# Two-layer hybrid encoder trunk: residual with tokens on partitions, hand-over between sub-layers by token block, next sub-layer begun on half of the tokens

## The reference

```python
for l in range(DEPTH):
    f = swiglu(rms_norm(x, ffn1_pre_g[l]), ffn1_w_gate[l], ffn1_w_up[l], ffn1_w_down[l])
    x = x + 0.5 * rms_norm(f, ffn1_post_g[l])
    m = hybrid_mixer(rms_norm(x, mix_pre_g[l]), ...)      # MLA, GLA, retention, one output projection
    x = x + rms_norm(m, mix_post_g[l])
    f = swiglu(rms_norm(x, ffn2_pre_g[l]), ffn2_w_gate[l], ffn2_w_up[l], ffn2_w_down[l])
    x = x + 0.5 * rms_norm(f, ffn2_post_g[l])

def rms_norm(x, g):
    return x * lax.rsqrt(jnp.mean(x * x, axis=-1, keepdims=True) + EPS) * g
def swiglu(x, w_gate, w_up, w_down):
    return (jax.nn.silu(x @ w_gate) * (x @ w_up)) @ w_down
```

## Time and profile before

| | |
|---|---|
| Median of 3 runs | 2079.45 us (2075.5 to 2079.79) |
| Profiled execution | span 2078.5 us from first to last instruction; the runs' own times stand in the line above |
| TensorE products / weight loads busy | 97% / 78% |
| VectorE, ScalarE, POOL busy | 43%, 33%, 9% |
| Mean granted TensorE clock | 0.982 |
| Read from HBM | 172.79 MB, 84 GB/s over the span |

### The profile page before, as it was taken

The page is one execution under the profiler, slowest core; times in us unless marked ns, Lnnn a source line. Parts: engine busy times, 40 slices in busy tenths (PEclk is TensorE's granted clock), DMA queues, the critical chain, the costliest instruction groups (busy, mean ns, idle before and its releaser), DMA issues.

```text
span 2078.5 us, 25293 instructions
## 1 busy us (share of the span) xinstructions
PE 2020.5 (97%) x9540; PEld 1628.4 (78%) x9540; DVE 897.6 (43%) x1137; ACT 693.5 (33%) x901; POOL 179.4 (9%) x185
## 2 busy tenths in 40 slices
PE   7999999999999999999999999999999999999997
PEld 6888888696677888888778888886956778888885
DVE  3444422635445544431364444226354464444314
ACT  5322211524443423221252223124444343223212
POOL 2000000202222000000020000003032220000000
PEclk9999999999999999999999999999999999999998
DMA  4222222230012222222212222223200112222222
GB/s 165 102 83 98 101 101 92 90 109 21 1 42 81 82 101 99 85 98 101 102 62 102 86 96 101 101 95 115 72 11 21 41 61 102 101 101 93 89 101 81
DMA packets 26615, 176.01 MB, mean 85 GB/s; under 512 B 3330, under 2 KB 3492, under 8 KB 6308
## 3 DMA queue, kind: packets, MB, share of 16 engines
q1 hardware_dynamic: 25024, 170.03, 22.4%
q10 hardware_dynamic: 1508, 4.87, 0.7%
HBM read 172.79 MB, written 2.10 MB: 84 GB/s over the span
## 4 chain that ended last, share of the span: by engine, by line
issue 77%; PE 16%; POOL 5%; DVE 1%; ACT 1%; DMA 0%; POOLq 0%; SPq 0%; DVEq 0%; ACTq 0%
POOL xL L1474 3%; PE ps L365 2%; PE ps L367 2%; PE ps L366 2%; PE ps L600 1%; PE ps L707 1%; POOL rstd L1484 1%; PE ps L725 1%; PE ps L518 1%; PE ps L519 1%; PE ps L520 1%; PE ps L714 0%; PE ps L609 0%; PE ps L641 0%; PE ps L682 0%
## 5 line engine op out<-in xcount | busy, mean ns | idle before, releaser
L1115 DVE TENSOR_TENSOR WL<-raw,WH 128x2048 fp32r<-128x2048 f32 x152 | 348.3, 2292 | 722.7 <-ACT WH L836 722.7
L365 PE MATMUL ps<-xH,WH 128*128 128x512 f32 x1632 | 639.3, 392 | 0.0
L367 PE MATMUL ps<-xH,WL 128*128 128x512 f32 x1632 | 635.4, 389 | 0.0
L366 PE MATMUL ps<-xL,WH 128*128 128x512 f32 x1632 | 635.3, 389 | 0.0
L836 ACT ACTIVATE WH<-raw 128x2048 fp32r<-128x2048 f32 x156 | 298.8, 1915 | 675.1 <-PE ps L367 675.1
L367 PEld LDWEIGHTS ps<-xH,WL 128*128 128x128 f32 x1632 | 306.1, 188 | 64.8
L365 PEld LDWEIGHTS ps<-xH,WH 128*128 128x128 f32 x1632 | 306.1, 188 | 64.4 <-issue 1.0
L366 PEld LDWEIGHTS ps<-xL,WH 128*128 128x128 f32 x1632 | 306.2, 188 | 63.8 <-issue 1.0
L366 PE MATMUL ps<-hL,WH 128*128 (+1 forms) x704 | 273.9, 389 | 0.0
L367 PE MATMUL ps<-hH,WL 128*128 (+1 forms) x704 | 273.9, 389 | 0.0
L365 PE MATMUL ps<-hH,WH 128*128 (+1 forms) x704 | 273.9, 389 | 0.0
(11 more groups left out here) (224 smaller groups left out, 1712.4 us busy)
## 6 DMA issues: line engine op xcount, KB each, us to landing
raw<-stream SPq DMA_DIRECT2D x158, 1024.0 KB, 4.8
x<-x_in SPq DMA_DIRECT2D x4, 512.0 KB, 9.7
wq<-w_q_up ACTq DMA_DIRECT2D x4, 512.0 KB
out<-x SPq DMA_DIRECT2D x8, 256.0 KB, 2.1
const<-consts ACTq DMA_DIRECT2D x2, 578.5 KB
wkv<-w_kv_up ACTq DMA_DIRECT2D x2, 512.0 KB
cos<-positions ACTq DMA_DIRECT2D x2, 256.0 KB
gains_all<-gains_in SPq DMA_DIRECT2D x1, 79.5 KB, 4.9
```

The lines of the kernel that those rows point to most:

```text
L365: mm(dst, wh, xh, start=start, stop=False)
L366: mm(dst, wh, xl, start=False, stop=False)
L367: return mm(dst, wl, xh, start=False, stop=stop)
L1115: tt(WL[:, slot, :], raw[:, slot, :], WH[:, slot, :].bitcast(F32), ALU.subtract).then_inc(wL_ready, 1)
```

## The change

The residual now has tokens on partitions: x is 4 blocks of 128 tokens by 1024 features. The down and output projections swap operands (hidden tile stationary, weights moving), so that two banks hold one token block. The mean of squares is then a sum along a row, which ScalarE's square delivers with it; POOL takes the power of one column per block; `residual` and `normed` scale by a column and by a gain row that a transfer has repeated over all partitions. Each normed block is turned by 8 transposes (`turn_block`) into two banks, from which ScalarE and VectorE make xH and xL (`high_x`, `low_x`). The next norm is fully applied ahead of the projections, so the multiplications by rstd_x go, and with them `columns`, the spreads of the eight outer norms, and `busy`.

The last two pairs of a sub-layer run together, output bank by output bank (`last_pairs`), so that token blocks are finished one after the other. The next sub-layer's first two pairs run on the first half of the tokens and then on the second (`enter`, `half_pair`), with the turns of blocks 2 and 3 in between. A third weight slot, used by pair base alone (`slot_of`), lies over gate, up and other tiles that rest at that time. Both layers are written out instead of looped. x comes in and leaves as 4 blocks. The core of the diff, with "..." where lines are left out:

```diff
-FFN_START = [2, 3, 6, 7, 4, 5, 0, 1]
+FFN_START = [6, 7, 2, 3, 4, 5, 0, 1]
...
+def slot_of(i):
+    return 2 if i == 0 else (i - 1) % 2
...
+            def load_norm_gains(k):
+                for j, row in enumerate((2 * k, 2 * k + 1)):
+                    if 0 < row < 2 * STAGES + 1:
+                        sp.dma_start(norm_g[:, j, :], norm_gains[row].partition_broadcast(P)).then_inc(norm_g_landed, 16)
+            sp.dma_start(x[:, 0, :], x_in[:, 0, :]).then_inc(x_landed[0], 16)
+            load_norm_gains(0)
+            sp.dma_start(ident[:], consts[:, C_ID:C_ID + P]).then_inc(ident_landed, 16)
+            sp.dma_start(x[:, 1, :], x_in[:, 1, :]).then_inc(x_landed[1], 16)
+            load_pair(0)
+            for b in range(2, BLK):
+                sp.dma_start(x[:, b, :], x_in[:, b, :]).then_inc(x_landed[b], 16)
+            load_pair(1)
...
+            for stage in range(STAGES):
+                base, pairs = first_pair_of(stage), MIX_PAIRS if stage % 3 == 1 else FFN_PAIRS
+                for p in range(base, base + pairs):
+                    if p < 2:
+                        continue
+                    sp.wait_ge(wH_ready, p - 1)
+                    sp.wait_ge(wL_ready, p - 1)
+                    if p == base + FT + 6:
+                        sp.wait_ge(pair_done, base + FT + 2)
+                        load_norm_gains(stage + 1)
+                    load_pair(p)
+                if stage % 3 == 1:
+                    sp.wait_ge(q_psum, HEADS * (stage // 3 + 1))
+                    sp.wait_ge(k_psum, HEADS * (stage // 3 + 1))
+                    load_norm_gains(stage + 1)
+            for b in range(BLK):
+                sp.wait_ge(x_ready, BLK * (STAGES - 1) + b + 1)
...
+            def turn_block(stage, b):
+                pe.wait_ge(xn_ready, BLK * stage + b + 1)
+                for t in range(DT):
+                    last = nc.tensor.transpose(ps[:, 2 * b + t // 4, t % 4 * P:(t % 4 + 1) * P],
+                                               xn[:, b % 2, t * P:(t + 1) * P], ident[:])
+                    if b == 1 and t == 0 and stage:
+                        last.then_inc(pair_done, 1)
+                last.then_inc(x_turned, 1)
+            def half_pair(slot, banks, half, widths, middle):
+                tok = slice(half * SEQ // 2, (half + 1) * SEQ // 2)
+                for k in range(DT):
+                    if k in middle:
+                        turn_block(*middle[k])
...
+                    for j in range(2):
+                        at = j * SLAB + k * P
+                        last = three(ps[0:widths[j], banks[j], tok], wH(slot)[:, at:at + widths[j]],
+                                     wL(slot)[:, at:at + widths[j]], xH[:, k, tok], xL[:, k, tok],
+                                     k == 0, k == DT - 1)
+                return last
+            def enter(stage, base, widths=(P, P)):
+                if stage == 0:
+                    turn_block(0, 0)
+                    turn_block(0, 1)
+                wait_pair(base)
+                pe.wait_ge(xH_ready, BLK * stage + 2)
+                pe.wait_ge(xL_ready, BLK * stage + 2)
+                half_pair(2, (0, 1), 0, (P, P), {})
+                wait_pair(base + 1)
+                half_pair(0, (2, 3), 0, widths, {3: (stage, 2), 5: (stage, 3)})
+                pe.wait_ge(xH_ready, BLK * stage + 4)
+                pe.wait_ge(xL_ready, BLK * stage + 4)
+                half_pair(2, (0, 1), 1, (P, P), {}).then_inc(pair_done, 1)
+                half_pair(0, (2, 3), 1, widths, {}).then_inc(pair_done, 1)
+            for layer in range(DEPTH):
                 due = counter(layer)
...
-                def down_tile(p, slot, d, moving, first, last_pair):
+                def down_tile(slot, d, held, first, last_pair):
+                    b, half = divmod(d, 2)
+                    tok = slice(b * P, (b + 1) * P)
                     for j in range(2):
-                        at = j * SLAB + d * P
-                        h, l = moving[j]
-                        last = three(ps[:, d, :], WH[:, slot, at:at + P], WL[:, slot, at:at + P], h, l,
+                        cols = slice(j * SLAB + half * SEQ, j * SLAB + (half + 1) * SEQ)
+                        h, l = held[j]
+                        last = three(ps[:, d, :], h[:, tok], l[:, tok], WH[:, slot, cols], WL[:, slot, cols],
                                      first and j == 0, last_pair and j == 1)
-                    if last_pair and d != F_ORDER[-1]:
-                        last.then_inc(f_ready, 1)
                     return last
...
+                def last_pairs(stage, p, slots, held):
+                    wait_pair(p)
+                    wait_pair(p + 1)
+                    for d in range(2 * BLK):
+                        if stage < STAGES - 1 and d == 6:
+                            turn_block(stage + 1, 0)
+                        last = down_tile(slots[0], d, held[0], False, False)
+                        if d == 2 * BLK - 1:
+                            last.then_inc(pair_done, 1)
+                        down_tile(slots[1], d, held[1], False, True).then_inc(f_ready, 1)
+                    if stage < STAGES - 1:
+                        turn_block(stage + 1, 1)
+                def ffn(stage, f_stage, base):
...
+                    down_pair(base + FT, slot_of(FT), hidden(0), True, order=FFN_START, emptied=n0 + FT)
+                    down_pair(base + FT + 1, slot_of(FT + 1), hidden(2), False)
+                    for n in range(2, 9):
+                        down_pair(base + FT + n, slot_of(FT + n), hidden(2 * n), False)
+                    last_pairs(stage, base + FT + 9, (0, 1), (hidden(18), hidden(20)))
...
+                def high(p, m, raw_slot, slot):
+                    act.wait_ge(landed[raw_slot], 16 * (m + 1))
+                    act.wait_ge(pair_done, p - 1)
+                    af(WH[:, slot, :], raw[:, raw_slot, :], ACT.Copy).then_inc(wH_ready, 1)
+                def high_at(base, i):
+                    high(base + i, (base + i) // 2, (base + i) % 2, slot_of(i))
+                def high_first(stage, base):
+                    if stage % 3 == 2:
+                        act.wait_ge(o_gated, due(o_gated, 4))
+                    elif stage:
+                        act.wait_ge(hL_ready, FT * (stage - stage // 3))
+                    act.wait_ge(landed[base % 2], 16 * (base // 2 + 1))
+                    af(WH2[:], raw[:, base % 2, :], ACT.Copy).then_inc(wH_ready, 1)
+                def high_next(stage, base, i):
+                    act.wait_ge(landed[(base + i) % 2], 16 * ((base + i) // 2 + 1))
+                    if stage:
+                        act.wait_ge(f_ready, 2 * BLK * stage)
+                    af(WH[:, slot_of(i), :], raw[:, (base + i) % 2, :], ACT.Copy).then_inc(wH_ready, 1)
+                def square_f(stage, b):
+                    for d in (2 * b, 2 * b + 1):
+                        act.wait_ge(f_ready, 2 * BLK * (stage - 1) + d + 1)
+                        if b:
+                            act.wait_ge(sum_f_ready, 2 * BLK * (stage - 1) + d - 1)
+                        af(squares[:, 0, d % 2 * SEQ:(d % 2 + 1) * SEQ], ps[:, d, :], ACT.Square,
+                           scale=1.0 / (32.0 * SHARES[(stage - 1) % 3]),
+                           accum_out=sum_f[:, d:d + 1]).then_inc(sum_f_ready, 1)
+                def square_x(stage, b):
+                    if stage:
+                        act.wait_ge(x_ready, BLK * (stage - 1) + b + 1)
+                    else:
+                        act.wait_ge(x_landed[b], 16)
+                    if b:
+                        act.wait_ge(sum_x_ready, BLK * stage + b)
+                    af(squares[:, 1, :], x[:, b, :], ACT.Square, scale=1.0 / 32.0,
+                       accum_out=sum_x[:, b:b + 1]).then_inc(sum_x_ready, 1)
+                def high_x(stage, b):
+                    act.wait_ge(x_turned, BLK * stage + b + 1)
...
+                    af(block_of(xH, b), turned_block(b), ACT.Copy).then_inc(xH_ready, 1)
+                def enter(stage, base):
+                    if stage == 0:
+                        square_x(0, 0)
+                        square_x(0, 1)
+                        high_first(0, base)
+                        high_x(0, 0)
+                        high_x(0, 1)
+                        square_x(0, 2)
+                        square_x(0, 3)
+                        high_next(0, base, 1)
+                    else:
+                        high_first(stage, base)
+                        square_f(stage, 0)
+                        square_f(stage, 1)
+                        square_x(stage, 0)
+                        square_f(stage, 2)
+                        square_x(stage, 1)
+                        high_x(stage, 0)
+                        square_f(stage, 3)
+                        high_x(stage, 1)
+                        high_next(stage, base, 1)
+                        square_x(stage, 2)
```

(125 more changed lines are left out.)

628 lines of the change are left out of this document (241 added, 387 removed).

## The result

| | before | after |
|---|---|---|
| Median | 2079.52 us (4 runs) | 2095.47 us (4 runs) |
| Ratio, 95% interval | | 1.0082 (1.0066 to 1.0099) |
| Profiled execution | span 2078.5 us | 2093.1 us, span 2091.1 us |
| Mean granted clock | 0.982 | 0.987 |

The kernel is 0.8% slower; the forecast was 2096 us. One of the four runs after, disturbed at 2276.69 us, is left out of the ratio; the others lie between 2093.1 and 2096.52. The total fits by luck, not term by term: a cost that I had put at nothing is about as large as what I put too high elsewhere.

What follows compares the result with a forecast made beforehand. The prediction took TensorE to bound the kernel. Hand-overs +18.5, start +5.1 and end -7.2 us summed to +16.4, added to the median 2079.45 for 2096 us; range 2076 to 2116.

Steps and rivals of the forecast that it cites:

- Stall: Before each sub-layer's last two pairs, TensorE has nothing for 4.5 us while pair FT+10 is split; six times.
- the clock behind it: After the stall the clock falls, costing the following products 2.3 us, with bounds 1.7 and 3.4.
- Chain of the blocks: Hand-over steps block by block end at 55.6 us; with stall and clock 63.6 against 59.9, +3.7, five times +18.5.
- The wait for WL: In the hand-over TensorE idles 3.0 us before pair base+1, waiting for its low half from VectorE.
- a second fall of the clock: In each hand-over a second gap may lower the clock again; 1.2 us, part absorbed by the wait for WL.
- 4 x 0.15 x 4 = 1.5 us: Extra time in a hand-over for 192 half products, 0.12 us each against 0.227/2.
- the fillers: In the old hand-over they brought the clock back sooner than in the mixer, so a fall was taken as 2.3 us.
- Swap of operands at nothing: Down products swap stationary and moving operand, both taken as 128 by 512 as before; no cost.
- Start and end: Kernel start +5.1 us, as x, a gain row and block 1 load before weights; end 36.8 against 44.0, -7.2 us.
- rival 1: The clock holds through the stall and later gaps, so not slower: -3.4 us, 2076 us; chance 0.15.
- rival 2: Longer hand-over chain: VectorE's 1024-column steps take 1.6 us and roots 1.0; +14, 2110 us; chance 0.17.
- rival 3: The clock falls twice or more in each hand-over, unabsorbed, +2.3 to 2.8 us more each; +12, 2108 us; chance 0.17.

Runs made afterwards that it cites:

- e3: The kernel after with pair FT+8 (in the mixer pair IN+1) in the third weight slot, so both last pairs can be split beforehand: 2060.2 us (0.9911).
- e9: The kernel after with 160 bytes per partition added ahead of the hidden tiles, so they begin at 512n + 128 as the weights do: 2081.8 us (1.0018).
- e12: The kernel after with the hidden tiles moved by 416 bytes per partition to 512n + 384, weights still at 512n + 128: 2082.7 us (1.0021).
- e11: e4 with VectorE's low half of pair base+1 brought forward, block 1 turned ahead of bank 7, and block 3 turned one feature tile sooner: 2023.5 us (0.9733).
- e4: The kernel after with the third weight slot of e3 and the 160 bytes of e9 together: 2045.6 us (0.9848).
- e2: The kernel before with weights WH and WL moved 32 bytes to 512n + 160; the hidden tiles moved too, to 512n + 192: 2120.9 us (1.0209).

## Why the prediction came out right, point by point

- **Stall.** 4.5 us predicted, 4.48 measured, six times; the clock behind it 2.3, measured 1.6 to 2.6 (products that start more than 0.27 us apart, less 0.2267 each). Shown by e3.
- **Chain of the blocks.** Turn 0 is 0.2 us late where I had 1.1 (0.4 in the mixers, whose products are not slower): the chain was some 0.4 to 0.7 shorter, and the slower products took 0.5. The 2.5 us before the first half are 2.46. The wait for WL is 2.0 and not 3.0 us, and in the first hand-over what a second fall of the clock costs is taken from it, as foreseen. For the clock I had 3.5 us in a hand-over; measured are about 2.6 (2.1 on average behind the stall, and some 1.4 more in two of the five). A hand-over is 61.7 us with the 0.7 of slower products in three of five, against 63.6: +1.4 without them, not +3.7. These three terms, each priced too high, make up the difference.
- **Two slips that move no sum.** The working "4 x 0.15 x 4 = 1.5 us" for the half products is wrong; 192 products by 0.0067 are 1.3, and the chain used 5.8 us for a half, which holds them. And I read the fillers as having brought the clock back sooner than in the mixer; by the earlier trace rows it stood at 0.50 for 6.8 us in both places. The 2.3 us taken for a fall still lies within what the stalls show.
- **Swap of operands at nothing.** This is the step that failed, by about 15 us. The swap itself costs nothing, as the mixer and e9 show (0.2267 us), but I did not look at where the tiles lie once the list ahead of them changes. (The stationary tile of a product is 128 by 128, not 128 by 512 as I wrote.)
- **Mixers.** -5.3 us that I had no term for. 5.1 of it is clock, and 3.4 of that lies behind the one-column products, which dropped the clock in the first mixer before and not after (window 462.5 to 465). That is chance and no effect of the change: in the same execution of the kernel before, the second mixer ran these products at the full clock, and in e12, whose mixer is that of the kernel after, the first mixer dropped it. Of before (second mixer) and of e12:

```profile
1480.00:1482.50 2.50, 2.50 (x24) 2.50 (x24) 0.04 (x1) 2.48 (x6) 0.00 (x0) 1.00 0.00 0
```
```profile
460.00:462.50 2.50, 2.50 (x13) 2.50 (x13) 0.23 (x2) 2.46 (x4) 1.65 (x1) 0.50 0.00 0
```

- **Start and end.** +4.4 for +5.1, and -7.9 for -7.2.
- **Rivals.** The clock didn't hold (rival 1). VectorE's steps took 1.28 and 1.22 us (rival 2 had 1.6). A second fall came in three of five hand-overs at 1.7 us of clock each, so rival 3 is half there, but behind waits and not behind transposes alone: in e11 turns 0 and 1 stand between products with less than 0.5 us of idle time and turn 2 behind a wait of 1.54, and the clock is 1.00 in every window from 375 to 397.5. The Trainium skill ("TensorE: Matmul & The Clock Gate", Part 4) says that transposes don't count as busy the way products do; in e11 that cost nothing at 1 us of transposes at a time. What longer stretches do, no run here shows.

In sum: 16.4 predicted, + 15.0 for the slower products (12.1 in the bodies, 2.9 in the last pairs), - 11.4 in the hand-overs (7.1 without their slower products, for 18.5), - 5.3 in the mixers, - 0.7 at the start, - 1.4 at the end (-8.6 without its slower products) = 12.6 us, the difference between the spans. The cost that I missed was covered, by luck, by the hand-overs that I priced too high and by the clock in the mixers. With the tiles of e9, at 2081.8 us, the same forecast would have been 14 us too high.

## What to carry to other kernels

When a list of tiles changes, look at the spacing of a product in the trace before and after, also in places the change doesn't touch: 3% on the down products alone were 0.6% of this kernel. A new dependence that joins two steps (here two pairs at once) needs a buffer more, or it pays in front what it saves behind. In a pipelined hand-over, write down for each engine which instruction stands ahead of the one TensorE waits for: a few exchanges in three lists gave back 22 us (e11 against e4) without taking any work away.

## What the runs showed of the hardware that I had not expected

- A product of 512 columns starts 0.2267 us behind the last, or 0.2324 to 0.2342 us, by where its operands begin in SBUF; both the moving and the stationary operand matter. All fast cases have tiles at 128 modulo 256 bytes. Products of 256 columns stayed at 0.12 us in e2, the one run that moves an operand of theirs.
- About 3 us of one-column products lowered the clock to 0.50 in one mixer of the kernel before and not in the other, in one execution of the same code.
- A stall of 4.48 us on TensorE was followed by a clock of 0.50 all six times; waits of 2.0 to 2.5 us only in some hand-overs (three of five in the kernel after).
